# Two transformer blocks in emulated fp32 on one core: how each stage starts from the one before

## What is computed

```python
def rms_norm(x, g):
    y = x * lax.rsqrt(jnp.mean(x * x, axis=-1, keepdims=True) + EPS)
    return y * g

def conv_glu_ffn(xn, w_up, conv_w, w_down):                 # up: 1024 x 5632, down: 2816 x 1024
    u = causal_dwconv(xn @ w_up, conv_w)
    g, val = jnp.split(u, 2, axis=-1)
    return (jax.nn.silu(g) * val) @ w_down

def first_block(x, ...):
    x = x + even_mixer(rms_norm(x, even_norm), w_in, ..., w_out)
    x = x + conv_glu_ffn(rms_norm(x, ffn_norm[0]), ...)
    x = x + retention_mixer(rms_norm(x, odd_norm), wq, wk, wv, wg, gn_gain, wo)
    return x + conv_glu_ffn(rms_norm(x, ffn_norm[1]), ...)

def stick_breaking_attention(q, k, v):                      # 8 heads of 64
    z = einsum('bqhd,bkhd->bhqk', q, k) * scale
    log_1m = where(strict, -softplus(z), 0.0)
    later = lax.cumsum(log_1m, axis=3, reverse=True) - log_1m
    w = where(strict, exp(log_sigmoid(z) + later), 0.0)
    return einsum('bhqk,bkhd->bqhd', w, v)

def second_block(x, ...):
    for l in range(2):
        h = rms_norm_2(x, g_pre_mix[l])
        qkv, gates = h @ w_in[l]
        y = g_a * (nsa_attention(...) @ w_proj_nsa) + g_b * (stick_breaking_attention(...) @ w_proj_sb)
        x = x + rms_norm_2(y @ w_out[l], g_post_mix[l])     # the norm comes before the sum
        f = conv_ffn(rms_norm_2(x, g_pre_ffn[l]), ...)
        x = x + rms_norm_2(f, g_post_ffn[l])
    return x
```

## Time and profile before

| | us |
|---|---|
| median of three runs (least, most) | 3174.0 (3173.13, 3176.74) |
| the profiled execution | 3175.93 |
| its span in the trace | 3174.2 |
| PE busy | 3043.8 (96%) |
| DVE, ACT, POOL busy | 1739.5, 1262.6, 470.8 |
| share of the chain that ended last: PE, DVE, ACT, issue | 88%, 6%, 4%, 2% |

### The profile page before, as it was taken

How to read it: one execution, slowest core, us unless ns; L and a number is a source line. 1 busy time by engine, 2 the same in 40 slices (tenths; PEclk the granted TensorE clock), 3 DMA queues, 4 the chain that set the end, 5 groups by cost and what they waited for, 6 DMA issues and landing times.

```text
span 3174.2 us, 37889 instructions
## 1 busy us (share of the span) xinstructions
PE 3043.8 (96%) x14560; PEld 2392.6 (75%) x14560; DVE 1739.5 (55%) x2998; ACT 1262.6 (40%) x2430; POOL 470.8 (15%) x452
## 2 busy tenths in 40 slices
PE   8999999999999999999999898999899998989997
PEld 6677888877777788888766676888677666768886
DVE  4555775345554577435454556773454545567743
ACT  3344443322333344332455534443223555344431
POOL 1201111111111111112002112111121011131110
PEclk9999999999999999999999999999999999999998
DMA  3222323222222233333211122232222111223332
GB/s 137 73 87 78 101 93 101 98 80 76 78 79 83 86 100 98 100 95 100 78 36 34 53 86 74 93 100 100 73 88 87 34 39 42 87 70 97 100 100 66
DMA packets 71604, 260.36 MB, mean 82 GB/s; under 512 B 7936, under 2 KB 7936, under 8 KB 71296
## 3 DMA queue, kind: packets, MB, share of 16 engines
q1 hardware_dynamic: 70128, 252.41, 24.7%
q10 hardware_dynamic: 1296, 5.52, 0.5%
HBM read 255.81 MB, written 2.10 MB: 81 GB/s over the span
## 4 chain that ended last, share of the span: by engine, by line
PE 88%; DVE 6%; ACT 4%; issue 2%; POOL 1%; DMA 0%; POOLq 0%; ACTq 0%; DVEq 0%
PE bank L421 24%; PE bank L425 23%; PE bank L422 23%; PE bank L564 2%; PE bank L594 2%; PE bank L488 2%; PE bank L492 2%; PE bank L489 2%; PE bank L575 1%; PE bank L702 1%; DVE wl L1245 1%; PE bank L810 1%; ACT pp L1190 1%; DVE x L1619 1%; PE bank L840 1%
## 5 line engine op out<-in xcount | busy, mean ns | idle before, releaser
L421 PE MATMUL bank<-xh,wh 128*128 128x512 f32 x2528 | 1027.1, 406 | 63.6 <-ACT wh L890 25.6
L425 PE MATMUL bank<-xh,wl 128*128 128x512 f32 x2528 | 996.0, 394 | 3.7 <-DVE wl L1245 2.4
L422 PE MATMUL bank<-xl,wh 128*128 128x512 f32 x2528 | 993.9, 393 | 0.0
L1245 DVE TENSOR_TENSOR wl<-ring,wh 128x512 fp32r<-128x512 f32 (+1 forms) x708 | 559.8, 802 | 740.2 <-ACT wh L890 738.4
L890 ACT ACTIVATE wh<-ring 128x512 fp32r<-128x512 f32 (+1 forms) x944 | 564.6, 619 | 641.5 <-PE bank L425 571.0
L421 PEld LDWEIGHTS bank<-xh,wh 128*128 128x128 f32 x2528 | 480.6, 190 | 221.5 <-ACT tmp L901 54.0
L1801 POOL TENSOR_TENSOR wl<-ring,wh 128x512 fp32r<-128x512 f32 (+1 forms) x236 | 308.4, 1307 | 2203.7 <-ACT wh L890 2203.7
L425 PEld LDWEIGHTS bank<-xh,wl 128*128 128x128 f32 x2528 | 479.7, 190 | 110.9 <-DVE wl L1245 5.6
L422 PEld LDWEIGHTS bank<-xl,wh 128*128 128x128 f32 x2528 | 481.4, 190 | 94.5 <-issue 3.8
L421 PE MATMUL bank<-bigr,wh 128*128 128x512 f32 x960 | 375.4, 391 | 5.2 <-DVE bigr L1546 4.9
L425 PE MATMUL bank<-bigr,wl 128*128 128x512 f32 x960 | 374.4, 390 | 0.0
(11 more groups left out here) (195 smaller groups left out, 2703.9 us busy)
## 6 DMA issues: line engine op xcount, KB each, us to landing
ring<-in_w_up SPq DMA_DIRECT2D x176, 512.0 KB, 3.4
ring<-in_w_down SPq DMA_DIRECT2D x88, 512.0 KB, 3.5
ring<-in_w_in SPq DMA_DIRECT2D x64, 512.0 KB, 3.5
...
```

The source lines that it names most:

```text
L421: e.matmul(o, K.wh(p, c, 128), oh, start=start, stop=False, skip_group_check=True)
L422: e.matmul(o, K.wh(p, c, 128), ol, start=False, stop=False, skip_group_check=True)
L425: m = e.matmul(o, K.wl(p, c, 128), oh, start=False, stop=stop, skip_group_check=True)
L1245: e.tensor_tensor(K.wl(i, 0, w), K.raw(i), K.wh(i, 0, w).bitcast(F32), ALU.subtract).then_inc(F.lo.tell(("piece", i)), 1)
```

## The change

- **Start.** x(0) comes in a transfer of its own at the head of SP's queue, the eight gains in one of 128x8 ahead of the other vectors on ACT's queue, and ACT loads its function table before it waits for either.
- **Groups.** `up` and `n` begin five tiles together, `ro` three over its 16 chunks, `r` still four; the weights in memory are laid out for that. In a group each step takes the two matmuls by `xh(k)` of all tiles first, then the matmuls by `xl(k)` of all tiles. In every other tile the order within a chunk is high by high, low by high, high by low.
- **Norms.** No diagonal: PE spreads the factors itself, in four matmuls of 128 columns whose stationary operand repeats a column of four numbers. In `e` the spread stands at chunk 5 of the tile behind the group, in late groups at chunk 4 with the sums at 0.
- **Borders.** `eo` to `f0` prescales x(j) at once, as the others did; `eo` reads split operands in `bigr`, the convolution's first. ACT squares the tiles of `wo` and `down` out of PSUM, and DVE makes `xl` of step k behind the sum of step k+1. At the end three of the eight sums go to POOL.
- **`n`.** `rope(5)` stands behind the compressions' first product.
- **Stick-breaking.** `sph` stands before the exponentials on ACT; the split of four of `y`'s eight operands stands at step 17, ahead of the last copy.

```diff
 # PE: three matmuls of a chunk are now high(...) and low(...)
+    def high(o, p, c, oh, start):
+        if c == 0:
+            q.wait_ge(F.hi, ("piece", p))
+        e.matmul(o, K.wh(p, c * 128, 128), oh, start=start, stop=False, skip_group_check=True)
+        if c == 0:
             q.wait_ge(F.lop if p % 4 == 3 else F.lo, ("piece", p))
...
+        e.matmul(o, K.wl(p, c * 128, 128), oh, start=False, stop=False, skip_group_check=True)
...
+    def group(key, nk, operand, banks, hooks):
+        for k in range(nk):
+            oh, parts = operand[0](k), []
+            for m, b in enumerate(banks):
...
+                parts.append(take())
+                high(BK[b][:, :], *parts[m], oh, k == 0)
+            ol = operand[1](k)
+            for m, b in enumerate(banks):
+                low(BK[b][:, :], *parts[m], ol, k == nk - 1, *([("tile", *key, m)] if k == nk - 1 else []))
...
-    def spread(s, slot, b, freed, event):
-        q.wait_ge(F.dve, ("diag", s))
+    def spread(s, at, b, freed, event):
+        q.wait_ge(F.pool, ("rsn", s))
...
-        e.matmul(BK[b][:, :], K.cs("ones"), K.tmp(slot), start=True, stop=True).then_inc(F.stat.tell(("spread", s)), 1)
+        for i in range(NQ):
+            m = e.matmul(BK[b][:, i * 128:(i + 1) * 128], bc(K.SM[:, at + i:at + i + 1], [[0, 128]]), K.cs("ident"),
+                         start=True, stop=True, skip_group_check=True)
...
-        group(("up", f, "g"), 4, xn(s), {} if late else norm(s))
+        group(("up", f, "g"), DT, xn(s), [next_bank() for _ in range(5)], {} if late else norm(s))
-        for i in range(4, 2 * FT):
-            tile(("up", f, i), DT, xn(s), F.dve, norm(s, late=True) if late and i == 4 else {})
+        for i in range(5, 2 * FT):
+            tile(("up", f, i), DT, xn(s), F.dve, norm(s, 0, 4) if late and i == 5 else {})
...
 # ACT
+    e.preload_act_table_set("natural_log_exp_and_others")
...
-        group(("up", f, "g"), 4, feed, {} if late else {3: lambda: rs_row(s)})
+        group(("up", f, "g"), 5, feed, {} if late else {3: lambda: rs_row(s)})
         if late:
-            hi_for(("up", f, 4))
+            hi_for(("up", f, 5))
             rs_row(s)
         for i in range(2 * FT):
-            if i >= 4:
+            if i >= 5:
                 hi_for(("up", f, i))
             begin(i)
...
-    residual(("ro",), ("f", 1), True, {3: lambda: None, 6: ret_last})
+    group(("ro", "g"), 3, nothing, {7: ret_last}, 16)
+    residual(("ro",), ("f", 1))
...
-            q.wait_ge(F.dve, ("freed", *key, j))
+            q.wait_ge(F.proj, ("tile", *key, j))
             if j >= 3:
                 q.wait_ge(F.dve, ("sqa", s, j - 2))
-            square(s, j, M[j])
+            square(s, j, K.bank((*key, j))[:, :])
...
 # DVE
     def late_norm(s, key):
         lo_to(W.first[key] + 3)
         mean_square(s, DT * 128)
-        lo_to(W.first[key] + 4)
-        diagonal(s, 3, 224)
...
             e.tensor_tensor(K.x(j), K.x(j), M[j], ALU.add).then_inc(F.dve.tell(("x", nxt, j)), 1)
-            if nxt:
+            if j:
+                prescale(nxt, j - 1)
+            if j == DT - 1:
                 prescale(nxt, j)
```

More of the change, by code:

```diff
@@ L679, in ret_spread @@
     def ret_spread(h):
-        spread(("rh", h), 4, 4, F.dve, ("of", h, 3))
-    group(("r", "g"), 4, xn(s), norm(s))
+        spread(("rh", h), 64, 4, F.dve, ("of", h, 3))
+    last = [turn[0][(turn[1] - 1 - i) % 6] for i in range(6)]
+    group(("r", "g"), DT, xn(s), sorted((4, 5, 6, 7), key=lambda b: -last.index(b)), norm(s))
+    turn[0] = [5, 6, 7]
     by_token(("rv", 0), 512, s, F.act)
@@ L1198, in scalar_program @@
                             F.act.tell(("sph", l, n)), 1)
+                for n in pair:
+                    a = K.pr(n)[:, 0:S - kt * 128]
+                    q.wait_ge(F.dve, ("zmin", l, n))
+                    e.activation(a, a, ACT.Exp, bias=0.0, scale=1.0).then_inc(F.act.tell(("zexp", l, n)), 1)
                 for n in pair:
@@ L1211, in scalar_program @@
                         F.act.tell(("w", l, n)), 1)
+            if t == 17:
+                q.wait_ge(F.proj, ("tile", "gm", l, 15))
+                split(("y", l), [(K.NQT[j], F.act, ("on", l, j)) for j in range(4)], 0)
             if 0 <= t - 2 < 16 and (t - 2) % 4 == 3:
@@ L1587, in ret_stats @@
         mean_square(("rh", 3), 512, 4)
-        diagonal(("rh", 3), 4, 64)
     def ret_last():
```

353 lines of the change are left out of this document (185 added, 168 removed).

## The result

| | before | after |
|---|---|---|
| median (least, most), us | 3173.57 (3172.5, 3176.74), 4 runs | 3129.49 (3128.15, 3131.55), 4 runs |
| ratio to before, 95% interval | | 0.986 (0.9843, 0.9877) |
| span of the profiled execution | 3174.2 | 3126.4 |
| PE busy | 3043.8 (96%) | 3033.7 (97%) |

The change made the kernel 44.1 us faster in the median; 44.0 had been forecast, from a sum of thirteen terms. The spans of the two profiled executions differ by 47.8, of which 37.7 are time in which PE stood still (130.4 before, 92.7 after) and 10.1 busy time. That the total is met to a tenth is luck: single terms were off by up to 3.3 us, and they cancel. Engine names are as before, the lines are those of the changed kernel: L436 high by high, L439 low by high, L443 high by low; L944 `wh`, L1293 `wl`, L951 `xh`, L1301 `xl`.

A forecast was written before the change was run, and what follows sets the result against it. PE, busy 96% of the span, was taken as the bound, so only its idle time and lower clock could change. Thirteen terms sum to -44.0 us, from the 3174.0 median to 3130.0; range for 8 in 10: 3108 to 3150.

The forecast's parts named there:

- The start: Kernel start: smaller first transfers and an earlier table load bring PE's first matmul from 13.74 to 9.5; -4.2 us.
- Stick-breaking: Both layers: with `sph` first, `spl` follows the caps directly, saving 9.7 us a layer; -19.4 us.
- Late groups: Groups of f2, f3 and layer 1's `n`: PE starts earlier, DVE's loop sets 4.6 us a step; -13.5 us.
- the slower rival: Groups: four weight slots for five chunks make each step wait for itself, 6.7 us for 4.6; 3180 us, 5%.
- Ramps behind f0 and f1: Behind both groups PE waits for a later `wh`, 7.1 us idle at worst plus clock loss; +6.2 each, +12.4 us.
- The first norm: In `e`, the spread's 1.4 us wait for the diagonal goes, less 0.3 for the squares; -1.1 us.
- third rival: Behind f0's and f1's groups: the ramps do not grow, silu and second product being reached in time; 3117 us, 15%.
- `ro` and `n`: `ro` as a group keeps 5.1 of a 9.3 us loss, -4.2; `rope(5)` moved in `n` costs 0.9 a layer, +1.8.
- The end: Kernel end: thirteen DVE instructions take 2.1 less, start 1.4 earlier, POOL's sums give back 0.5; -3.0 us.
- The lower end of the bound (1.4): Kernel end: if each of three POOL sums holds up one of DVE's by 0.7, the gain is 1.4, not 3.0.

The follow-up runs named there:

- its own experiment: Changed kernel with ACT making `sph` behind the exponentials again in stick-breaking: 3150.9 us, ratio to before 0.9922.
- the experiment: Changed kernel with each chunk's three matmuls done together within a group, PE waiting for `xh(k)` and `xl(k)` before a step: 3157.85 us, ratio to before 0.9944.

## Why the prediction was right, and where it was not

**The start** gave 3.6 for 4.2. ACT's first `xh` is at 7.14 for 10.70, directly behind the table load (5.84, 1.28 us) and the issues of ACT's transfers. The data are no longer what ACT waits for, but the load still lies in its way.

**Stick-breaking** was the largest term and is shown by its own experiment: 9.8 us less waiting a layer, against 9.7 forecast; of twelve waits eight are gone altogether, and the longest falls from 2.9 us to 1.7. The stretches with `y` gave 14.4 and 15.3, of which 11.7 and 11.4 are idle time (mainly the 9.8, and 2.0 for the first operand of `y`, less 0.5 for a new wait) and 2.6 and 3.9 busy time, with a granted clock of 1.00 for 0.99 and 0.99 for 0.98.

**Late groups.** The sum came out (-3.9, -6.7, -2.6 against -3.8, -7.8, -3.8), and the step is 4.6. But the reason given for the step was wrong, and its size came out by luck. I argued that DVE's loop sets the pace. In the changed kernel DVE works 3 us of a step and waits 1.6 for `wh` (timelines of PE, POOL, ACT and DVE):

```profile
1885.53 1.43 PE L443 MATMUL bank<-xl,wh 128*128 128x512 f32 x5 [0.90 <-DVE xl L1301]
1886.16 1.29 POOL L1941 TENSOR_TENSOR tmp<-tmp 128x512 f32<-128x512 f32 x1 [3.29 <-ACT tmp L955]
1886.36 0.63 ACT L944 ACTIVATE wh<-ring 128x512 fp32r<-128x512 f32 x1 [0.27 <-PE bank L443]
1887.02 0.98 DVE L1293 TENSOR_TENSOR wl<-ring,wh 128x512 fp32r<-128x512 f32 x1 [1.55 <-ACT wh L944]
1887.93 0.73 DVE L1656 SCALAR_TENSOR_TENSOR big<-big,vec,bank 128x512 f32<-128x512 f32 x1
1888.70 0.69 DVE L1659 TENSOR_TENSOR x<-x,big 128x512 f32<-128x512 f32 x1
1889.31 0.74 DVE L1301 SCALAR_TENSOR_TENSOR xl<-x,vec,xh 128x512 fp32r<-128x512 f32 x1
1890.11 1.43 PE L443 MATMUL bank<-xl,wh 128*128 128x512 f32 x5 [0.89 <-DVE xl L1301]
```

But for POOL's line each follows the one before, round to PE: it is the loop through the slots for weights that the slower rival describes, to which I gave 5%, only with fewer of PE's matmuls in it. With more of them in it, in the experiment, the step is 5.3 to 6.6 us and the kernel 28 us slower. A second path ends almost together with it: sum, `xh`, square, POOL's add, DVE's split. The split ends 0.55 us behind POOL's add (1888.00 and 1887.45), as it did before (1901.84 and 1901.30), though it starts 0.86 us behind POOL's start here and 0.47 there. Where POOL is not at work it takes 0.69, and would end some 0.3 sooner. That path is as long in both kernels, and so the step is 4.6 in both. This is read from the timelines; no run moved POOL's add.

**Ramps behind f0 and f1.** +6.2 each was forecast: 7.1 idle at worst, 7.0 measured (6.4 and 0.6). The clock of 0.92 over the 63 us of the window costs 5 us, where 3.3 were put in; f1's stretch came out at 5.0. The fifth tile causes most of it (four tiles: 3.5 us; before: 2.5). That reading of ACT's program, by counting what stands ahead of the next `wh`, is the step of the prediction that I would trust most in another kernel. The prediction's third rival, that the ramps do not grow, is out.

**The first norm** is the term that failed: -1.1 forecast, +2.2 measured. I followed the wait that goes (the diagonal) and took 0.3 off for the squares; 0.75 us remained, and behind it the clock was at its lower level for twice as long: the window 36:50 has 0.76, and 0.88 in the kernel before. Its row could not be seen in the trace of before, and no term of the sum had a bound for a longer stretch at the lower clock.

**`ro` and `n`.** `ro` gave 2.1 more than forecast. The four outputs of the last head (from 964.79 to 975.24 now) are nearly covered: PE waits 2.1 us for the `wh` behind them, at 975.90, and 0.2 for its low part, and the clock over 930:985 is 1.00. So 2.3 of the 9.3 lost in the earlier trace rows are left, none of it clock, where I had left 5.1. In `n` PE waits 0.6 for a low part behind the group, 0.9 for `wh` behind the compression and 0.9 for DVE a little later, where the kernel before had one wait of 0.7: +2.7 for the +0.9 of moving `rope(5)`. It looks like the cause of the ramps again, a helper engine late with the next piece, but no run tests it.

**The end** gave 5.1 for 3.0. DVE starts 4.50 us behind PE's last matmul of `down` for 6.84 (3160.56), 2.3 earlier where 1.4 were forecast. Its thirteen instructions take 8.36 and not 9.1, since two products in a row cost 0.67 each, and no sum of DVE was held up. The lower end of the bound (1.4) rested on the Trainium skill (SBUF — State Buffer, Who interferes with whom), by which the second of the two engines to issue is blocked. The trace agrees with that rule, but the second one here is POOL: it starts 0.16 us behind DVE's sum and takes 1.65 where its squares took 1.33. That is 0.3 more, and less than the 0.53 that were left of DVE's sum. What the rule costs depends on who is first, and I had only asked what it costs if DVE is second.

**The total** of 3130.0 against 3129.5 is then a sum of misses of +0.6, +3.3, -1.1, -2.1, -1.2, +1.8, -2.7, -0.1, +1.1, -1.6, +1.2, -2.1 and -1.0, which together are, but for rounding, -3.8 in the profiled executions, and the medians moved 3.7 less than these. The range of 42 us was meant for such errors; a forecast to half a microsecond was not to be had by this method.
